# Second projection: three row blocks first, then six column blocks by one level of Strassen's algorithm in two passes over the tokens

## The reference, cut to what matters

```python
h = rmsnorm(h_res, norm_w) * (1.0 + scale) + shift          # 2048 x 1024
proj = h @ w_in + b_in                                      # 1024 x (9 * 512 + 16)
(na_q, na_k, na_v, na_z, ml_q, ml_k, ml_v, ml_o, ml_z, i_f, f_f, i_b, f_b) = split(proj)
na_out = neighbourhood_attention(na_q, na_k, na_v, rpb) * silu(na_z)
qk = silu(centred_short_conv([ml_q, ml_k], conv_w, conv_b))  # 5 taps along the tokens
h_fwd, h_bwd = mlstm_chunkwise(mq, mk, mv, gates), the same backwards
hm = (h_fwd + h_bwd) * sigmoid(ml_o); ... * silu(ml_z)
out = concatenate([na_out, ml_out]) @ w_out
```

## Time and profile before

| | |
|---|---|
| median of 3 runs (lowest to highest) | 1960.67 us (1959.12 to 1961.04) |
| the profiled execution: time, span | 1959.82 us, 1957.5 us |
| PE busy, share of the span | 1897.9 us, 97% |
| DVE, ACT, POOL busy | 981.1, 626.7, 590.0 us |
| share of PE in the chain that ended last | 86% |
| DMA, mean | 155 GB/s |
| mean granted clock of TensorE | 0.991 |

### The profile page before, as it was taken

The page is one execution under the profiler, slowest core; times in us unless marked ns, Lnnn a source line. Parts: engine busy times, 40 slices in busy tenths (PEclk is TensorE's granted clock), DMA queues, the critical chain, the costliest instruction groups (busy, mean ns, idle before and its releaser), DMA issues.

```text
span 1957.5 us, 26466 instructions
## 1 busy us (share of the span) xinstructions
PE 1897.9 (97%) x9913; PEld 1549.6 (79%) x9913; DVE 981.1 (50%) x2099; ACT 626.7 (32%) x1316; POOL 590.0 (30%) x967
## 2 busy tenths in 40 slices
PE   6999999989999899999999999999998999799998
PEld 5888878768888788888888687888886776688887
DVE  6564565664676533113777222123213776576665
ACT  5421212122444432101222112221113666555552
POOL 3122333122652211100100000222214777544442
PEclk9999999999999999999999999999999999899999
DMA  5232333345887765312222123665564566856663
GB/s 177 79 101 73 99 97 100 104 139 182 280 296 215 235 199 164 118 49 86 70 71 76 41 63 114 194 216 170 169 206 126 179 206 225 288 194 232 237 221 113
DMA packets 240571, 303.53 MB, mean 155 GB/s; under 512 B 41526, under 2 KB 164310, under 8 KB 240412
## 3 DMA queue, kind: packets, MB, share of 16 engines
q1 hardware_dynamic: 213004, 215.84, 36.3%
q0 software_dynamic: 25136, 81.81, 11.4%
q10 hardware_dynamic: 2304, 4.20, 0.6%
HBM read 194.71 MB, written 107.54 MB: 154 GB/s over the span
## 4 chain that ended last, share of the span: by engine, by line
PE 86%; POOL 4%; DVE 3%; DMA 3%; issue 2%; ACT 1%; SPq 0%; POOLq 0%; DVEq 0%; ACTq 0%
PE banks L145 25%; PE banks L147 24%; PE banks L146 24%; PE banks L1854 2%; PE banks L1836 2%; PE banks L2410 2%; PE banks L1817 2%; PE banks L2412 1%; PE banks L2145 1%; POOL p L1786 1%; PE banks L2380 1%; POOL e L1787 1%; POOL mid L1766 1%; PE banks L231 1%; PE banks L955 1%
## 5 line engine op out<-in xcount | busy, mean ns | idle before, releaser
L145 PE MATMUL banks<-hT,wu 128*128 128x512 f32 x512 | 201.7, 394 | 1.5 <-DVE hT L217 1.5
L147 PE MATMUL banks<-hT,wu 128*128 128x512 f32 x512 | 200.1, 391 | 0.0
L146 PE MATMUL banks<-hT,wu 128*128 128x512 f32 x512 | 199.9, 390 | 0.0
L145 PE MATMUL banks<-iT,wua 128*128 128x512 f32 x384 | 151.5, 394 | 2.2 <-DVE iT L1258 2.2
L145 PE MATMUL banks<-iT,wub 128*128 128x512 f32 x384 | 151.3, 394 | 1.9 <-DVE wub L1258 1.9
L145 PE MATMUL banks<-wub,iT 128*128 128x512 f32 x384 | 150.5, 392 | 0.0
L146 PE MATMUL banks<-iT,wua 128*128 128x512 f32 x384 | 150.2, 391 | 0.0
L147 PE MATMUL banks<-iT,wua 128*128 128x512 f32 x384 | 150.1, 391 | 0.0
L147 PE MATMUL banks<-iT,wub 128*128 128x512 f32 x384 | 149.7, 390 | 0.0
L146 PE MATMUL banks<-wub,iT 128*128 128x512 f32 x384 | 149.5, 389 | 0.0
L147 PE MATMUL banks<-wub,iT 128*128 128x512 f32 x384 | 149.4, 389 | 0.0
(11 more groups left out here) (283 smaller groups left out, 4188.5 us busy)
## 6 DMA issues: line engine op xcount, KB each, us to landing
iraw<-in_w_in SPq DMA_DIRECT2D x36, 512.0 KB, 4.3
wa<-in_w_ada SPq DMA_DIRECT2D x48, 256.0 KB
raw<-in_pool_in_w SPq DMA_DIRECT2D x16, 512.0 KB, 4.2
yT<-sg POOLq DMA_DIRECT2D x32, 256.0 KB, 3.0
oraw<-yT SPq DMA_DIRECT2D x32, 256.0 KB, 5.4
xr<-in_x SPq DMA_DIRECT2D x16, 512.0 KB, 4.5
h<-h POOLq DMA_DIRECT2D x16, 512.0 KB, 3.8
hT<-tr POOLq DMA_DIRECT2D x16, 512.0 KB, 5.1
```

What stands on the lines that cost most here:

```text
L145: e.matmul(ps, lh, rh, start=first, stop=False)
L146: e.matmul(ps, lh, rl, start=False, stop=False)
L147: return e.matmul(ps, ll, rh, start=False, stop=last)
```

## The change

`Proj` is replaced by two classes. `Rows` does mv, nv with the gates, and mo, with the same units of 24 matmuls of 128x512; only the first four tiles of mv are made in two halves of 256 columns. mo takes tiles 8 to 15 first. `Columns` then does the six column blocks in 24 groups. A group is 256 output columns x 1024 tokens. It is one 2x2x2 product of quadrants with K = 512 each, and Winograd's form of Strassen's algorithm makes seven products of quadrants in the place of eight: 7 x 4 K tiles x 3 = 84 matmuls of 128x512 in the place of 96. Groups 0 to 11 take the first 1024 tokens, groups 12 to 23 the others, so each column of weights is loaded in two passes.

The seven weight operands `A[s]` (four are sums of quadrants: `s_sum`, on POOL) are split anew for each group, high on ACT, low on POOL (0, 2, 3, 1) and DVE (4, 5, 6). Each has one buffer; the buffer of operand s is free when product s of the group before is done. The seven token operands `B[s]` are made twice: during mo's last eight tiles (`t0_*`, from 1 MB loads through one raw buffer), and at the turn, group 11 (`TURN - 1`), when the products of group 11 set them free (`t_sum`, `t_split_high`, `t_split_low`). The products go round five PSUM banks. DVE combines the partial results (`partial`: t2, t3, u3; `result`: C22, C11, C12, C21), seven instructions a group, each reading one bank. The taps of the convolution are now 1022 to 1026 wide; the first is ACT's, the other four for each of two channel tiles are DVE's, in the group behind.

The steps of `Gates` stand at products 0, 2, 3 and 5 of groups 1 to 5, those of `States` at the same places of groups 16 to 23 (`ticks`). The attention's first loads are issued at products 0, 1, 2 and 4 of the last group.

```diff
-BLOCKS = [("nq", 0), ("nk", 1), ("mv", 6), ("mk", 5), ("mq", 4), ("nv", 2), ("nz", 3), ("mz", 8), ("mo", 7)]
-class Proj:
+ROW_BLOCKS = [("mv", 6), ("nv", 2), ("mo", 7)]
+class Rows:
...
+        work = [("mv", m, c) for c in range(2) for m in range(4)] + [("mv", m, 2) for m in range(4, NT)]
+        work += [("nv", m, 2) for m in range(4)] + [("gates", tb, 2) for tb in range(TB)] + [("nv", m, 2) for m in range(4, NT)]
+        self.mo_order = [*range(8, NT), *range(8)]
...
+        ahead = {0: [("w", 2)], 1: [("w", 3)], 2: [("h", 1, 0)], 3: [("h", 1, 1)], 4: [("h", 1, 2)], 5: [("h", 1, 3)]}
+        for x in range(4):
+            ahead[9 + x] = [("h", 2, x)]
+            ahead[13 + x] = [("h", 3, x)]
+            ahead[17 + x] = [("w", 4 + x)]
...
+class Columns:
+    ORDER = [("mk", 5, 0), ("nq", 0, 0), ("mk", 5, 1), ("nq", 0, 1), ("mq", 4, 0), ("nk", 1, 0), ("mq", 4, 1), ("nk", 1, 1),
+             ("nz", 3, 0), ("nz", 3, 1), ("mz", 8, 0), ("mz", 8, 1)]
+    NG = 24
+    TURN, GATES0, STATES0 = 12, 1, 16
+    OUTS = [("C22", 3, 1, 1), ("C11", 4, 0, 0), ("C12", 5, 0, 1), ("C21", 6, 1, 0)]
+    LOW_POOL, LOW_DVE, HIGH = (0, 2, 3, 1), (4, 5, 6), (0, 2, 1, 3, 4, 5, 6)
...
+    def early_pool(self, e, w, i):
...
+        if i in (8, 10, 12, 14):
+            self.t0_sums(e, w, (i - 8) // 2)
...
+    def ticks(self, states, g, s):
+        if g == self.NG:
+            return (states.s0 + 32, states.s0 + 33) if s == 6 else ()
+        for g0, n0, top in ((self.GATES0, states.g0 - 1, 18), (self.STATES0, states.s0, 32)):
+            if g >= g0 and s in (0, 2, 3, 5):
+                t = 4 * (g - g0) + (0, 2, 3, 5).index(s)
...
+    def dve(self, e, w, states):
+        for g in range(self.NG + 1):
+            on, j, turn = g < self.NG, g + 1, g == self.TURN - 1
+            for s in range(7):
+                if s == 0:
+                    self.post_dve(e, w, g - 1, 3)
+                    self.other_taps(e, w, g - 1, 0)
+                if on:
+                    if s == 1:
+                        self.partial(e, w, g, "t2")
+                    if s == 2:
+                        self.partial(e, w, g, "t3")
+                        if turn:
+                            self.t_sum(e, w, 2)
+                    if s == 3:
+                        self.edges(e, w, g)
+                        self.result(e, w, g, 0)
+                        self.partial(e, w, g, "u3")
+                        if turn:
+                            self.t_sum(e, w, 3)
+                            self.t_sum(e, w, 1)
+                    if s == 4:
+                        self.post_dve(e, w, g, 0)
+                        self.result(e, w, g, 1)
+                        self.a_low(e, w, j, 4)
+                        if turn:
+                            self.t_split_low(e, w, 1)
+                    if s == 5:
+                        self.post_dve(e, w, g, 1)
+                        self.result(e, w, g, 2)
+                        if turn:
+                            self.t_split_low(e, w, 2)
+                    if s == 6:
+                        self.post_dve(e, w, g, 2)
+                        self.result(e, w, g, 3)
+                        self.keep(e, w, g)
+                        self.a_low(e, w, j, 5)
+                        self.a_low(e, w, j, 6)
+                        if turn:
+                            self.t_split_low(e, w, 3)
+                if s == 0 and g == self.TURN:
+                    self.t_split_low(e, w, 6)
+                if s == 3:
+                    self.other_taps(e, w, g - 1, 1)
+                for n in self.ticks(states, g, s):
+                    states.dve(e, w, n)
+
+    def pool(self, e, w, att, states):
...
+                if s == 2:
+                    self.s_sum(e, w, j, 1)
+                    self.s_sum(e, w, j, 2)
+                    self.a_low(e, w, j, 0)
+                    self.a_low(e, w, j, 2)
+                if s == 3:
+                    self.s_sum(e, w, j, 3)
+                if s == 4:
+                    self.a_low(e, w, j, 3)
+                    if turn:
+                        self.t_split_low(e, w, 4)
+                if s == 5:
+                    self.s_sum(e, w, j, 4)
+                    self.a_low(e, w, j, 1)
+                if s == 6 and turn:
+                    self.t_sum(e, w, 6)
+                for n in self.ticks(states, g, s):
+                    states.pool(e, w, n)
...
+    def pe(self, e, w, states):
+        for g in range(self.NG + 1):
+            for s in range(7):
+                if g < self.NG:
...
+                    self.low_done(w, g, s)
+                    self.b_ready(w, self.groups[g][0], s)
+                    a, b = self.A[s], self.B[s]
+                    for x in range(4):
+                        t = mm3(e, self.bank(g, s), a[:, 0, x], a[:, 1, x], b[:, 0, x], b[:, 1, x], x == 0, x == 3)
+                    t.then_inc(*self.full.inc())
+                for n in self.ticks(states, g, s):
+                    states.pe(e, w, n)
```

More of the change, by code:

```diff
@@ L1386, in act, with dve @@
-            states.act(e, w, n)
-    def dve(self, e, states):
-        out, bc, cw, cb = self.out, self.bc, self.cw, self.cb
-        w = Waits(e)
-        out.tail_dve(e, w, -1)
-        for n, (name, u, tb) in enumerate(self.work):
+            if self.tail_at(n) is not None:
+                out.tail_act(e, w, self.tail_at(n))
+            if cols:
+                cols.early_act(e, w, n - self.n_mo)
+    def dve(self, e, w, first, end, cols=None):
+        out = self.out
+        if first == 0:
+            out.tail_dve(e, w, -1)
+        for n in range(first, end):
+            name, m, c = self.work[n]
+            i = self.tile[n]
@@ new lines, in read_out, with pe @@
+    def read_out(self, w, i):
+        name, m = self.tiles[i]
+        if name == "gates":
+            w.wait_ge(*self.evac.ge(m + 1))
+        else:
+            w.wait_ge(*self.row_step.ge(self.row_at[i]))
+    def pe(self, e, w, first, end):
+        out = self.out
+        for n in range(first, end):
+            name, m, c = self.work[n]
+            i = self.tile[n]
+            if c != 1:
+                if i >= 8:
+                    self.read_out(w, i - 8)
+                elif i < 6:
+                    w.wait_ge(*out.added.ge(28 + 2 * (i // 2)))
+                else:
+                    w.wait_ge(*out.t_out.ge(2 * NT))
+            pb = self.pg(i)
@@ L1572, in __init__ @@
         self.st = k.at("ast", 119, [P, 128, 3])
-        nw = len(proj.work)
-        places = proj.reserved + proj.place[nw - 5:]
-        self.numbers, self.last = [proj.BANKS[i] for i in places], [proj.banks[i] for i in places]
+        own = [x % 5 for x in range(7 * cols.NG - 5, 7 * cols.NG)]
+        self.numbers = cols.reserved_no + [cols.ring_no[i] for i in own]
+        self.last = cols.reserved + [cols.ring[i] for i in own]
         self.pS, self.pT, self.pO = self.last[0:4], self.last[4:6], self.last[6]
@@ L2041, in sp @@
     def sp(self, e, w, n):
-        k, proj = self.k, self.proj
+        k, rows = self.k, self.rows
         if n == self.g0 - 1:
-            for i in range(2):
-                w.wait_ge(*proj.ca_st[i].ge(16))
-            proj.stored_all(w, "gates")
+            w.wait_ge(*rows.full.ge(len(rows.work)))
+            rows.stored_all(w, "gates")
             self.g.sp(e, w, 0)
@@ L2110, in pool @@
         if n == self.g0 - 1:
-            for i in range(2):
-                w.wait_ge(*self.proj.ca_st[i].ge(16))
+            w.wait_ge(*self.rows.full.ge(len(self.rows.work)))
             self.g.consts(e, w)
@@ L2130, in pe @@
         if n == self.g0:
-            for b in self.proj.reserved:
-                self.proj.read_out(w, max(x for x in range(self.proj.nv0) if self.proj.place[x] == b))
+            for i in self.cols.other_tiles:
+                self.rows.read_out(w, i)
         self.g.pe(e, w, n - self.g0)
@@ L2741, in act2 @@
                 w = Waits(e)
+                rows.act(e, w, mo, end, cols)
+                cols.act(e, w, states)
                 att.act(e, w, tail)
@@ L2756, in pe2 @@
                 w = Waits(e)
+                rows.pe(e, w, mo, end)
+                cols.pe(e, w, states)
                 att.pe(e, w, tail)
```

1188 lines of the change are left out of this document (799 added, 389 removed).

## The result

The change made the kernel slower: 2060.76 us median (2058.93 to 2063.5, 4 runs) against 1960.86 of the kernel before, a ratio of 1.0511 [1.0493, 1.053]. 1941 was forecast with a range up to 1970. The profiled execution has a span of 2059.7 us against 1957.5.

A forecast was written before the change was run, and what follows sets the result against it. PE, busy 97% of the span, was taken to bound the kernel by matmul count. -65 + 4 + 2 + 3 + 12 + 22 + 2 = -20 us on 1959.8, plus 0.9, gave 1941 us; range 1908 to 1970.

The forecast's parts named there:

- The -65 us: Six column blocks: 2304 matmuls become 2016, so 288 fewer at 0.226 us each save 65 us.
- The third rival: Products don't shorten PE: operands from a slower pattern would make the matmul pitch grow by 1/7; chance 0.02.
- the second, DVE as the bound: Rival: POOL instructions block DVE, 45 us a pair of groups, 64 against 48.6 with States; 1993 us; chance 0.16.
- States: +22: Groups 16 to 23: POOL's operand instructions delay the weighing, 14 us, updates behind taps 8; +22 us (4 to 45).
- the prediction's other wait: Groups behind mq: PE's step at product 5 waits for a state update behind taps, +4 us each, 8 in all.
- Gates: +3: Groups 1 to 5: PE's steps wait for DVE steps behind taps, two meetings of 1 to 2 us; +3 (0 to 8).
- The turn: +12: Groups 11 and 12: remaking B keeps DVE and POOL busy past product 3 of group 12; +12 us (8 to 20).
- The second sum of the prediction, with POOL: At the turn, DVE's 21 us and POOL's 26 us without overlap are 47 us between 2.7 and 35.4: +14.
- Hand-over: +2: Last group to attention: 7.2 MB of loads, then POOL builds `mid` after the table; +2 us (-2 to 11).
- Start, nv and B: +6: Start and nv +4 us (2 to 12), from 256-column matmuls and late splits; making B during mo +2 (0 to 6).
- all high ends together: The high ends of the six cost terms, set against the -65 us of matmuls; +37 us.

The follow-up runs named there:

- e1: Changed kernel with SP's loads and store of a Gates or States step issued ahead of the other stores and weight load of the same product; 2034.4 us.
- e2: Changed kernel with POOL's steps of States and Gates moved ahead of its operand instructions of the same product; 2063.9 us.
- e13: e9 with POOL's weighing ahead of its operand instructions of the same product; 2015.2 us.
- e10: e9 with the forward half of States first, two or three steps to a group from group 13; 2028.3 us.
- e5: e1 with ACT issuing loads of skC and skT behind its wait for the transposes, POOL those of sv behind its weighing; 2033.7 us.
- e11: e10 plus e5's queues, steps of groups 17 to 23 at every second product, and SP's load of group 13 ahead of a store; 2005.2 us.
- e3: Changed kernel with DVE's four convolution taps cut from some 1024 columns to 4, instructions and waits kept; 2036.7 us.
- e7: e1 with DVE's steps ahead of the taps, POOL's low parts of B4 behind A1's, and SP's load for group 13 ahead of a store; 2044.1 us.
- e9: e6 with Gates at products 1 and 5 of groups 1 to 9, and POOL's twelve low parts and four sums at the turn on DVE; 2019.2 us.
- e4: Changed kernel with the attention's first loads issued after the last group, not within it; 2070.4 us.
- e6: e1 with the attention's 16 q and k loads issued four at a time behind products 0 to 3, then table, v and z; 2031.1 us.
- e8: e1 with POOL making its first two operand sums of each group twice; 2089.8 us in one run.

## Why the prediction was wrong

The measured change of the span is +102 us, where -20 was forecast.

**The -65 us were right.** 288 matmuls are gone and the pitch stayed: groups 1, 7, 9, 10, 11 and 15 take 19.0 us. The third rival is false. So is the second, DVE as the bound: groups 7 and 15, behind one of mq and one of mk, hold no step and take 19.0. (In this rival's sum 64 against 48.6 is 15.4, not 16 a pair, which moves it by 1 us.) The meetings themselves cost: four low parts on DVE take 6.77 us beside POOL and 2.49 alone. The Trainium skill ("SBUF — State Buffer", section "SBUF: two separate sides") says that the loser of the shared ports waits for the whole instruction. The rows of the turn agree, 6.77 against 2.49. But in the groups without steps DVE had room for the meetings.

**States: +22, the step that failed.** It cost 79 us in groups 16 to 22 alone. The prediction let POOL's four operand instructions set the step and took the load of `skC` as landing "inside the same stall". It costed that load from when PE was done, 3.2 us, and never asked what stands ahead of it in SP's program: a weight load that waits for DVE's last low part, stores that wait for DVE and ACT. e1 gives 30 us for that; e2, which removes the predicted cause, gives nothing as long as the load is later than POOL (only group 22 falls, from 25.7 to 22.8). With SP's loads ahead, POOL's order costs 4.5 us a group in groups 21 and 22 (e13), against the 1.8 that the prediction had. Its mechanism was right as the second layer, and sized low: an operand instruction of POOL takes 1.30, not 1.07, the wait is 2.7 us, and the slower clock behind it adds 1.8. Durations of POOL's two instructions in the kernel after, ns min/median/max:

```profile
L1631 POOL TENSOR_TENSOR A<-As,A x72: 1262/1301/2308, 867.7 to 1541.9; 128x512 fp32r<-128x512 f32 x72
L2782 POOL TENSOR_TENSOR swv<-sv,wT x30: 1046/1054/1197, 1322.4 to 1584.0; 128x516 f32<-128x516 f32 x30
```

Of the rest of groups 16 to 19, 19 us are group 16's: mk's last store leaves at 1311.0 us, 11 us into it, and the first `skC` can only be loaded behind it, for which PE waits 18.8 us in the kernel after and 13.8 in e1. The prediction had no term for this cold start. In e10 that wait is gone (group 16, with one step, 20.4), at the price of the same steps elsewhere. The other 16 us are in groups 17 to 19 (e1). Some 8 of them are pairs one product apart at 6.5 to 6.8 us instead of 4.1; the rest are waits for `skC`, `swv` and `state` at other places. The place of the loads in SP's queue (e5), POOL's order (e13) and the distance (e11) each left these groups no shorter. In e11 the prediction's other wait shows, for the update of `state` behind the taps, 5.7 us where it had 4; what sets the whole was not settled.

**Gates: +3, sized wrong.** Groups 0 to 11 have 28 us over, of which 2.6 are a wait for B and some 5 stood in the kernel before. Two meetings of 1 to 2 us were counted; two waits of PE are 8.1 and 5.2 (kernel after, 985 to 1050 us):

```profile
PE banks L2626 <- DVE L L2582: 8.1, 1, 8.1
PE banks L2638 <- DVE wT L2610: 5.2, 1, 5.2
```

DVE is behind by the taps (e3 takes 16 us off), and PE's step follows one product behind the DVE step it needs. Order inside the slot is no help (e7), distance is (e9: group 2 31.6 -> 20.1), though only 9 us in all.

**The turn: +12, sized wrong.** It took 30. The second sum of the prediction, with POOL, had it at +14 for 47 us of work that can't overlap. It took POOL's instructions at 1.07; they are up to 1.7 where DVE runs too, and POOL's low parts of B4 delay that of A1, which product 1 of group 12 waits 13.5 us for. e9, which gives POOL's sixteen instructions to DVE, gets back 6.

**Hand-over: +2, looked for in the wrong place.** The prediction asked only when the table would be there for the attention. Attention and tail take 2 us longer than before, as forecast. But the 16 loads and the step of States share SP's queue, and the store of `state` is slow to land among them: chain of the kernel after in the last group (start, length):

```profile
1565.04 0.65 SPq L2719
...
1566.31 12.05 DMA CD<-state
...
1579.14 2.06 PE banks L2801 x8
```

The update that this store waits for ends at 1553.1 us, so the store stands 13.2 us in SP's program behind the issues. Then it takes 12.05 us to land among 7 MB of loads, where it takes 3.5 elsewhere, and PE stands 22.2 us. The group costs 25 us. Without the loads in it (e4) it takes 24.2, so they are the cause; e6 returns 14 to the group and 3 to the whole, which its spread doesn't tell from nothing.

**Start, nv and B: +6, measured 9.5, in the terms' ranges.** Start and nv measured +7 against 4, B's low part is waited for 2.6 us against 2. The matmuls of 256 columns come every 0.12 us, as taken. At nv's first unit PE waits 2.0 us for `wset`, where the term had 1.9. Only the gap of the start did not quite stay: 7.9 us, 4.5 of them for `wset`, against 5.6.

Even all high ends together give +37. None of them had a queue in it: each was a duration set against a gap.

## What to carry to other kernels

When work is rewritten so that an engine's program order changes, write down for every load on a short loop what stands ahead of it in the queue that issues it, and what each of these waits for: here that was worth 26 us of the total and no duration in the old trace showed it. When the cover of a step is halved, read the closing time of its loops (here 4.4 to 5.0 us) before placing steps 4.1 us apart. Removing one cause can show the next (SP, then POOL in groups 21 and 22), so an experiment that finds nothing on the full kernel has to be made again once the layer over it is gone.

## What the runs showed that was not expected

- DVE and POOL, both making low parts of 128x512 with two SBUF sources, take turns one by one: four on DVE 6.77 us with POOL, 2.49 without; four on POOL 6.27, against 4 x 1.30.
- A wait costs more than its length: in group 21 of e1 PE waits 2.7 us for `swv` and the group is 4.7 us over its plan, with matmuls every 0.43 us behind the wait (granted clock 0.65 in the mean from 1480 to 1484 us, so in part at 1.2 GHz) before 0.23 again. Over the span the granted clock is 0.962 against 0.991.
- Two of POOL's 1.3 us instructions more in each group (e8) make a group without any step 1.3 us longer.
